# A two-block model on one core: where the squares of a stage's input rows are kept and summed, which blocks take the first half of the rows, and when a norm's reciprocal is taken

## The reference, cut to what matters

```python
def _rmsnorm(x, g):
    y = xf * lax.rsqrt(jnp.mean(xf * xf, axis=-1, keepdims=True) + RMS_EPS)
    return (y * g).astype(x.dtype)
...
for i in range(DEPTH):                                  # DEPTH = 2
    h = _rmsnorm(hres, norm_g[i, 0])
    m = _diff_attention(...) if i == 0 else _short_conv(...)
    hres = hres + _rmsnorm(m, norm_g[i, 1])
    h = _rmsnorm(hres, norm_g[i, 2])
    hres = hres + _rmsnorm(_sqrelu_mlp(h, w_up[i], w_down[i]), norm_g[i, 3])
...
z = rmsnorm(x, norm_gain) @ w_in                        # the second model: pooling, RWKV heads
x = x + y @ w_out; return rmsnorm(x, final_gain)
```

## Time and profile before

| | |
|---|---|
| median of 3 runs | 1658.22 us (1657.4 to 1659.14) |
| profiled execution | 1659.31 us, its span 1657.5 us, 1.8 us around it |
| PE busy | 1571.1 us, 95% of the span |
| DVE, ACT, POOL busy | 786.5, 620.3, 529.9 us |
| mean granted TensorE clock | 0.985 |
| share of PE in the chain that ended last | 69%, DVE 11% |

### The profile page before, as it was taken

The page is one execution under the profiler, slowest core; times in us unless marked ns, Lnnn a source line. Parts: engine busy times, 40 slices in busy tenths (PEclk is TensorE's granted clock), DMA queues, the critical chain, the costliest instruction groups (busy, mean ns, idle before and its releaser), DMA issues.

```text
span 1657.5 us, 31409 instructions
## 1 busy us (share of the span) xinstructions
PE 1571.1 (95%) x12656; PEld 1408.2 (85%) x12656; DVE 786.5 (47%) x1368; ACT 620.3 (37%) x1135; POOL 529.9 (32%) x235
## 2 busy tenths in 40 slices
PE   7999997999999999999999999999999989999895
PEld 6888886999999999989989888888889867777764
DVE  4333433654232231574445642332316799556655
ACT  5556665443222231332224432232324434433321
POOL 3122222134444444124431344444441244450020
PEclk9999999999999999999999999999999999999998
DMA  5121111222233322222222223232322122200001
GB/s 181 52 60 56 52 52 39 90 76 91 89 90 97 95 90 90 77 77 90 89 88 77 77 91 100 89 102 89 101 90 77 63 79 87 89 16 3 3 26 51
DMA packets 35401, 125.66 MB, mean 76 GB/s; under 512 B 3920, under 2 KB 4048, under 8 KB 35280
## 3 DMA queue, kind: packets, MB, share of 16 engines
q1 hardware_dynamic: 35280, 123.90, 23.5%
HBM read 121.79 MB, written 2.10 MB: 75 GB/s over the span
## 4 chain that ended last, share of the span: by engine, by line
PE 69%; DVE 11%; issue 2%; ACT 2%; DMA 0%; DVEq 0%; ACTq 0%; SPq 0%
PE G L1415 58%; PE G L1685 3%; PE ST L1685 3%; PE PV L1685 1%; PE ST L1388 1%; PE PO L1685 1%; DVE rstd L863 1%; DVE acc L1319 1%; DVE wlo L902 1%; DVE t L1169 0%; DVE z L1172 0%; DVE m L922 0%; DVE z L1161 0%; ACT rms L535 0%; PE PO L1415 0%
## 5 line engine op out<-in xcount | busy, mean ns | idle before, releaser
L462 POOL TENSOR_TENSOR wlo<-raw,whi 128x1024 fp32r<-128x1024 f32 x209 | 506.6, 2425 | 1085.0 <-ACT whi L511 645.9
L1415 PE MATMUL G<-xh,whi 128*128 128x258 f32 (+3 forms) x1504 | 372.8, 310 | 11.7 <-DVE t L1008 6.9
L1415 PE MATMUL G<-xl,whi 128*128 128x258 f32 (+3 forms) x1504 | 358.9, 301 | 0.0
L1415 PE MATMUL G<-xh,wlo 128*128 128x258 f32 (+3 forms) x1504 | 356.9, 300 | 0.0
L1415 PE MATMUL G<-ah,whi 128*128 128x256 f32 (+2 forms) x1024 | 279.3, 314 | 4.7 <-DVE al L1144 2.9
L1415 PE MATMUL G<-al,whi 128*128 128x256 f32 (+2 forms) x1024 | 277.6, 312 | 0.0
L1415 PE MATMUL G<-ah,wlo 128*128 128x256 f32 (+2 forms) x1024 | 277.4, 312 | 0.0
L521 ACT ACTIVATE whi<-raw 128x1024 fp32r<-128x1024 f32 x112 | 118.7, 1060 | 417.3 <-PE G L1415 411.6
L1415 PEld LDWEIGHTS G<-xh,whi 128*128 128x128 f32 x1504 | 245.0, 190 | 30.4 <-issue 11.5
L1415 PEld LDWEIGHTS G<-xl,whi 128*128 128x128 f32 x1504 | 244.8, 190 | 10.5
L1415 PEld LDWEIGHTS G<-xh,wlo 128*128 128x128 f32 x1504 | 245.2, 190 | 9.4
(11 more groups left out here) (306 smaller groups left out, 2027.6 us busy)
## 6 DMA issues: line engine op xcount, KB each, us to landing
raw<-weights_dram SPq DMA_DIRECT2D x225, 512.0 KB, 3.6
hres<-xT_dram SPq DMA_DIRECT2D x8, 264.0 KB, 5.8
out_dram<-hres SPq DMA_DIRECT2D x8, 256.0 KB, 2.1
con<-consts_dram SPq DMA_DIRECT2D x1, 512.0 KB, 7.6
mat<-mats_dram SPq DMA_DIRECT2D x1, 512.0 KB, 8.4
con<-consts_dram SPq DMA_DIRECT2D x1, 392.0 KB, 5.3
vec<-vecs_dram SPq DMA_DIRECT2D x1, 203.0 KB, 2.6
```

The source lines that it names most:

```text
L462: nc.gpsimd.tensor_tensor(wlo[:, s], raw[:, s % 2], whi[:, s].bitcast(F32), ALU.subtract)\
L1415: last_of[0] = nc.tensor.matmul(to[:, p0:p1], wt[:, w, ws], xt[:, k, t0 - off:t1_ - off], start=k == 0 and q == 0, stop=k == KT - 1 and q ...
```

## The change

1. The squares of a half row go to the row's own place in `m`, the old stage's result, whose half row has been added to `hres` by then. ACT no longer waits for `sq_used` in `input_square`.
2. PE sums the squares of all eight rows in one run, `sums(half)`, and no longer between rows.
3. In the first half, block 2 joins blocks 0 and 1: rows 0 to 3 for two blocks, then rows 0 to 3 of block 2, the two products of the norm after, rows 4 to 7 for three blocks, the run of sums, and block 3. In the second half: rows 0 to 3 for two blocks, rows 0 to 3 of block 2, rows 4 to 7 for two blocks, the run of sums, rows 4 to 7 of block 2, and block 3.
4. Block 4 of the first stage of an MLP and of the convolution waits for b - 2 blocks taken out, that is for block 1.
5. DVE takes the first half's reciprocal of the norm before after the second half's rows, and that of the norm after behind `low_w` of the fourth weight block; ACT takes the first half's root after two rows of the second half.
6. In the first chunk of an MLP DVE takes out block 1 before it makes the low part of block 0.

```diff
@@ post_squares (ACT)
-                    c = tokens(cols, half)
-                    if k + KT * half >= 4:
-                        act.wait_ge(sq_used, sq_base(s) + KT * half + k - 3)
-                    r, o = square_slot(k, half)
-                    nc.scalar.activation(t1[:, r, o:o + c.stop - c.start], hres[:, k, c], ACT.Square).then_inc(sq_ready, 1)
+                    nc.scalar.activation(squared_row(k, cols, half), hres[:, k, tokens(cols, half)], ACT.Square)\
+                        .then_inc(sq_ready, 1)
...
-                stat_root(s, cols, 0)
                 for k in range(KT + 2):
                     input_row(k, 1)
+                    if k == 1:
+                        stat_root(s, cols, 0)
                 stat_root(s, cols, 1)
@@ last_tiles (DVE)
                 input_rows((6, 7), 0)
-                stat_recip(s, cols, 1)
                 low_x(i + 1, *pre, KT - 1, cols, 0)
                 low_w(new + 3)
-                stat_recip(s + 1, cols, 0)
+                stat_recip(s, cols, 1)
                 dve.wait_ge(rstd_ready, stat_count(s, 1))
                 scaled(0, 1)
                 input_rows(range(KT), 1)
                 low_x(i + 1, *pre, KT - 1, cols, 1)
+                stat_recip(s + 1, cols, 0)
                 stat_recip(s + 1, cols, 1)
@@ mlp (DVE), first chunk
-                                up(b0 + UP[c] + j, j, (b0 + UP[c] + j) % 4)
+                                if j != 1:
+                                    evict(b0 + UP[c] + j, j, (b0 + UP[c] + j) % 4)
+                                if j == 0:
+                                    evict(b0 + UP[c] + 1, 1, (b0 + UP[c] + 1) % 4)
+                                low(j, (b0 + UP[c] + j) % 4)
@@ begin, first_blocks (PE)
-            def begin(b):
+            def begin(b, fifth=False):
...
-                    pe.wait_ge(tile_out, b - 1)
+                    pe.wait_ge(tile_out, b - (2 if fifth else 1))
...
+                start(0)
+                start(1)
+                for k in range(KT // 2):
+                    ready(k, 0)
+                    rows(0, [k], 0)
+                    rows(1, [k], 0)
+                start(2)
+                rows(2, range(KT // 2), 0)
+                post_stat(s - 1, cols, 1)
+                for k in range(KT // 2, KT):
+                    ready(k, 0)
+                    for j in range(3):
+                        rows(j, [k], 0)
+                sums(0)
+                start(3)
+                rows(3, range(KT), 0)
+                for k in range(KT):
+                    ready(k, 1)
+                    for j in range(2):
+                        rows(j, [k], 1)
+                        if k == KT - 1:
+                            done()
+                    if k == KT // 2 - 1:
+                        pe.wait_ge(rms_ready, stat_count(s, 0))
+                        rows(2, range(KT // 2), 1)
+                sums(1)
+                rows(2, range(KT // 2, KT), 1)
+                done()
+                pe.wait_ge(rms_ready, stat_count(s, 1))
+                rows(3, range(KT), 1)
+                done()
...
@@ product, body
-                    begin(b)
+                    begin(b, start is not None and isinstance(j, int) and j == HELD)
```

More of the change, by code:

```diff
@@ L126, in half_added @@
     return j + 1 + (HELD - 1 if half else 0)
-def square_slot(k, half):
-    q = k + KT * half
-    return q % 2, TOK // 2 * (q // 2 % 2)
 def held(cols, j, half):
@@ L277, in bank, with squared_row @@
                     PO[:], PV[:])[n]
+        def squared_row(k, cols, half):
+            return m[:, k, tokens(cols, half, cols[0])]
         def chunks(ap):
@@ L997, in low, with evict @@
                                 .then_inc(a_ready, 1)
-                        def up(b, j, s4):
+                        def evict(b, j, s4):
                             dve.wait_ge(block_done, b + 1)
@@ L1011, in up @@
                             last.then_inc(tile_out, 1)
+                        def up(b, j, s4):
+                            evict(b, j, s4)
                             low(j, s4)
@@ L1382, in stat_tile @@
                 for t0, t1_, p0, p1 in part(cols, half):
[L1383 to L1387, removed]
+                    squares = sq[:, k % 2, t0:t1_] if s == 0 else squared_row(k, cols, half)
                     last = nc.tensor.matmul(ST[:, p0:p1], ones, squares, start=k == 0, stop=k == KT - 1,
@@ L1436, in start, with ready, sums @@
                     pe.wait_ge(tile_out, b0 + j - 3)
[L1437 to L1440, removed]
+                def ready(k, half):
+                    pe.wait_ge(x_ready, x_base(i + 1) + KT * half + k + 1)
+                def sums(half):
                     for k in range(KT):
[L1442 to L1460, removed]
@@ new lines, in sums, with done @@
+                        stat_tile(s, k, cols, half)
+                def done():
+                    last_of[0].then_inc(block_done, 1)
+                start(0)
[11 more added lines that the diff above has]
+                        rows(j, [k], 0)
```

## The result

The changed kernel is slower: 1665.03 us, median of 6 runs (1663.16 to 1666.89), against 1657.49 us of 6 runs of the kernel before (1655.59 to 1659.14). The ratio is 1.0045, 95% interval 1.0033 to 1.0057. The profiled execution took 1663.51 us with a span of 1661.7 us, 4.2 us over the span before.

What follows compares the result with a forecast made beforehand. PE is busy 95% of the span, so only its waits and half clock count. Seams -1.56 + 1.89 + 0.58 + 2.10 = +3.0 us, with half clock at both MLPs +6.2 us: 1664.4 us by the median, 8-in-10 range 1656.5 to 1668.5 us.

Steps and rivals of the forecast that it cites:

- a sum in a run: On PE, each half row's sum of squares costs 0.43 us in a run, as between rows.
- new wait before block 2's rows: First half, first MLP: PE waits 1.06 us for block 2's low weights; the same new wait at the other seams.
- wait for row 7, gone: First half, first MLP: PE's 0.36 us wait for the seventh row goes, since PE comes there some 2 us later.
- net in the first half: First MLP seam: new wait less the wait for the seventh row, 1.06 - 0.36 = +0.70 us.
- the shift: Second half's root later by 12 products (1.42 us) plus the first half's net wait: 2.12 us into the first MLP.
- wait of block 5, its start: First MLP: block 5 waits 2.85 us for block 3 to be taken out, starting at 359.07 against 360.63 before.
- MLP 1, convolution, MLP 2, model 2: Changes at the four seams without half clock at the MLPs: -1.56, +1.89, +0.58, +2.10 us, together +3.0 us.
- half clock behind the MLPs' waits: PE at 1.2 instead of 2.4 GHz after block 5's wait in each MLP: +1.58 us each, +3.16 us at both.
- block 5 does wait: Judges the rival that block 5 doesn't wait, so block 4's early start pays in full: 1655.1 us, chance 0.12.
- sums are not cheaper in a run: Judges the rival that sums in a run cost a quarter less, 7 us over 64 half rows: 1657.5 us, chance 0.06.
- the new wait is there at all four seams: Judges the rival that the first half's new wait is nothing, 4.2 us less: 1660.2 us, chance 0.12.
- the longer half clock: Rival: half clock holds longer after the waits into the convolution and the second model: 1667.6 us, chance 0.12.

Runs made afterwards that it cites:

- e9: Kernel before with only the moves of the reciprocals and of the first half's root: median 1656.6 us, ratio 0.9989.
- e1: Changed kernel with all rows of block 2's second half behind the run of sums, so 48 products follow the last sum: median 1653.6 us, ratio 0.9979.
- e2: Changed kernel with block 2 joining the first half after row 4, not row 3, behind the norm's two products: median 1658.4 us, ratio 1.0000.
- e4: Changed kernel with ACT splitting block 4's weights ahead of the second half's root: median 1652.3 us, ratio 0.9966 to the kernel before.
- e11: Changed kernel with 20 extra products, changing no result, ahead of block 5's wait in both MLPs: median 1661.2 us, ratio 1.0021 to the kernel before.
- e5: Kernel before with squares in m and all eight sums in one run behind the rows, both halves: median 1669.2 us, ratio 1.0083.

## Why the prediction was right, step by step

The time forecast was 1664.4 us, measured 1665.0. The steps in the first MLP, and the sums:

| step | forecast | measured |
|---|---|---|
| a sum in a run | 0.43 us | 0.43 us |
| new wait before block 2's rows | 1.06 us | 1.09 - 0.12 + 0.10 = 1.07 us |
| wait for row 7, gone | 0.36 us | 0.63 us by e9 |
| net in the first half | +0.70 us | +0.45 us (349.99 against 349.52, less 0.02) |
| the shift | 2.12 us | 346.07 - 344.17 - 0.02 = 1.88 us |
| wait of block 4 | none | none |
| wait of block 5, its start | 2.85 us, 359.07 | 2.79 us, 358.90 |
| MLP 1, convolution, MLP 2, model 2 | -1.56, +1.89, +0.58, +2.10 | -1.75, +1.60, +0.25, +1.78 |
| half clock behind the MLPs' waits | +1.58 and +1.58 | +1.61 and +2.66 |

The mechanism held at each place. e1, e2 and e4 each took one link of it away, and the seams got shorter by what the link was said to cost, or a little more (5.8 us for 5.6, 4.4 for 3.1, 6.1 for 6). The times fell by more, 11.5, 6.6 and 12.8 us, because half clock went too. One term was mis-sized: the wait for the seventh row. I took the 0.36 us in brackets for it, but a wait in brackets starts at the modelled end of the last product, 0.28 us behind its start, so that the loss in PE's pace is larger; for the new wait I had counted from start to start. That made every seam 0.2 to 0.3 us too bad, 1.1 us in all. In the other direction half clock cost more than two times 1.58 us: behind the second MLP's wait it lasted longer. The two errors nearly cancel: the seams and the half clock behind the MLPs' waits come to 6.15 us, forecast 6.2. That the time came out within 0.6 us is so in part luck, and it depends on the runs too: the traced executions are 4.2 us apart and the medians 7.5 us, as half clock fell differently elsewhere too. The wait for row 7 also went for another reason than the prediction's first: it gave PE's later coming, and e9 loses the wait without it, by the reciprocal's move alone.

The rule of the Trainium skill (SBUF — State Buffer, section "SBUF: two separate sides") on the lock between DVE and POOL was used for the order of the low part and POOL. e4 tells it from a fixed cost: with less of POOL's work behind its start, the same instruction took 0.84 us instead of 1.55. The two orders in the convolution, under e11, agree with it in both directions: whichever of the two started first had its usual time, and the other was longer.

The rivals: block 5 does wait (2.79 and 3.28 us); sums are not cheaper in a run; the new wait is there at all four seams; the longer half clock, which I gave 0.12, was partly seen, into the second model and, where I hadn't put it, behind the second MLP, but not into the convolution.

One thing stands wrong in the text on the change: the eased wait doesn't reach the convolution either. From its fifth block on, that stage's block numbers come from a loop register, and the condition asks for a plain number. The changed kernel's trace shows it; block 4 waits there for block 2, for 0.24 us:

```profile
732.81 0.39 PE L1414 MATMUL G<-xh,whi 128*128 128x258 f32 x1 [0.24 <-DVE cb L1129]
```

The medians differ by 3.3 us more than the two profiled spans, and the granted clocks of the runs go with that; open stays at which places half clock fell in the runs that have no trace.

## What to carry to other kernels

Work of one engine that lies between two hand-overs of another is covered only there: collected into a run (e5), the same 0.43 us sums cost 12 us more in four seams, though each took as long as before. When a wait is eased, follow the next one behind it to its real start (here root, weight split, POOL, DMA, split, POOL, DVE), since a later root took back what the eased wait gave; moving one weight split ahead of the root (e4) took 6.1 us off the four seams, which the whole change had made 1.9 us longer. And price a wait by the starts of the products around it and by the clock behind it: the 2.8 us wait cost another 1.6 us afterwards. And a seam's length from one execution can turn on which of DVE and POOL starts first.

## What the runs showed of the hardware

- Waits of PE and the clock behind them, over the 13 traces of this case from 300 to 1400 us: of the idle times of 1.2 to 1.6 us none of 10 was followed by half clock, of 1.6 to 2.3 us 4 of 20, of 2.3 to 2.78 us 10 of 14, and of 2.78 to 5.1 us 38 of 42. The same wait of 2.45 us into the second model was followed by it in five traces and not in a sixth (e1). Ahead of 300 us each trace has two more such waits, of 1.3 and 1.6 us, that were not followed, and one of 2.2 us at which half clock had begun before the wait. So shortening a wait from 2.8 to 1.4 us can pay about twice: an estimate from the 1.4 us and the 1.61 us of half clock behind the first MLP's wait.
- Twenty products whose result nobody reads, put ahead of two waits of 2.79 and 3.28 us, left 0.41 and 0.84 us of idle time, and the granted clock behind was 1.00 at both (e11).
- A DVE instruction with two SBUF inputs that started while POOL made low weights ended some 0.55 us behind POOL at the places read here: the same low part took 0.84 us in e4 and 1.55 us in the changed kernel, by how long POOL still had to run. When DVE started first, it took its 0.69 us and POOL 2.78 us instead of 2.37 (e11).
